# Prologue of a differential-attention layer: modulation rows in two PSUM banks and partly on VectorE, the first weight group among x's tiles

## The reference, cut to what matters

```python
c_act = jax.nn.silu(c)
mod = c_act @ ada_w[0] + ada_b[0]                 # (1, 2048) @ (2048, 6144)
shift, scale, gate = jnp.split(mod, 3, axis=-1)
h = rms_norm(x, norm_pre[0]) * (1.0 + scale[:, None, :]) + shift[:, None, :]
y = diff_attention(h, diff_w_in, diff_w_out, ...)  # h @ diff_w_in first: (1024, 2048) @ (2048, 8192)
x = x + gate[:, None, :] * rms_norm(y, norm_post[0])
```

## Time and profile before

| what | value |
| --- | --- |
| median of 3 runs | 1999.75 us (1997.54 to 2002.05) |
| the profiled execution, own time | 2001.04 us |
| its span, first to last instruction | 1999.1 us |
| TensorE busy (PE) | 1943.5 us, 97% of the span |
| VectorE, ScalarE, GpSimd busy | 1282.0, 786.5 and 567.5 us |
| mean granted TensorE clock | 0.993 of full speed |

### The profile page before, as it was taken

The page is one execution under the profiler, slowest core; times in us unless marked ns, Lnnn a source line. Parts: engine busy times, 40 slices in busy tenths (PEclk is TensorE's granted clock), DMA queues, the critical chain, the costliest instruction groups (busy, mean ns, idle before and its releaser), DMA issues.

```text
span 1999.1 us, 26598 instructions
## 1 busy us (share of the span) xinstructions
PE 1943.5 (97%) x9252; PEld 1586.5 (79%) x9252; DVE 1282.0 (64%) x2096; ACT 786.5 (39%) x1567; POOL 567.5 (28%) x624
## 2 busy tenths in 40 slices
PE   5989999999999999999999999999999989999998
PEld 1368888888888877888888888888888878888886
DVE  1566676666566445778888887888878755534352
ACT  4433333333445332444444444444444434322240
POOL 1123333342456332333242423243332310000000
PEclk9999999999999999999999999999999999999999
DMA  9667666664365777776867777786868675476543
GB/s 327 199 221 242 211 203 204 207 191 142 138 216 200 247 284 242 226 238 200 255 207 238 231 223 229 217 249 207 249 196 256 221 266 167 129 253 201 162 153 85
DMA packets 391489, 426.52 MB, mean 213 GB/s; under 512 B 21078, under 2 KB 287420, under 8 KB 388796
## 3 DMA queue, kind: packets, MB, share of 16 engines
q1 hardware_dynamic: 391072, 424.76, 66.9%
q10 hardware_dynamic: 284, 0.05, 0.0%
HBM read 294.70 MB, written 130.03 MB: 212 GB/s over the span
## 4 chain that ended last, share of the span: by engine, by line
PE 90%; DVE 3%; issue 2%; SPq 2%; DMA 2%; POOL 1%; ACT 1%; DVEq 0%; POOLq 0%; ACTq 0%
PE ps L1545 28%; PE ps L1547 28%; PE ps L1546 28%; PE ps L1533 2%; PE ps L1663 2%; PE ps L1637 1%; POOL sums L724 1%; POOL stg L737 1%; PE ps L1521 1%; SPq L475 1%; PE ps L1682 1%; SPq L364 1%; DMA h_dr<-stg 1%; DVE ring L1110 0%; DMA x2s<-in_x_dram 0%
## 5 line engine op out<-in xcount | busy, mean ns | idle before, releaser
L1545 PE MATMUL ps<-blk,ring 128*128 128x512 f32 x1536 | 609.0, 396 | 11.8 <-ACT cc L889 5.1
L1547 PE MATMUL ps<-blk,ring 128*128 128x512 f32 x1536 | 600.4, 391 | 0.0
L1546 PE MATMUL ps<-blk,ring 128*128 128x512 f32 x1536 | 600.4, 391 | 0.0
L1545 PEld LDWEIGHTS ps<-blk,ring 128*128 128x128 f32 x1536 | 289.6, 189 | 71.9 <-issue 13.6
L1547 PEld LDWEIGHTS ps<-blk,ring 128*128 128x128 f32 x1536 | 289.6, 189 | 61.8
L1546 PEld LDWEIGHTS ps<-blk,ring 128*128 128x128 f32 x1536 | 290.0, 189 | 56.9
L1110 DVE TENSOR_TENSOR ring<-sums,ring 128x512 fp32r<-128x512 f32 x256 | 226.8, 886 | 127.6 <-ACT ring L820 125.4
L724 POOL TENSOR_TENSOR sums<-raw 128x512 f32<-128x512 f32 x128 | 193.1, 1509 | 365.4 <-DVE ring L1110 300.8
L820 ACT ACTIVATE ring<-sums 128x512 fp32r<-128x512 f32 x256 | 159.9, 626 | 177.8 <-PE ps L1547 177.8
L1110 DVE TENSOR_TENSOR ring<-raw,ring 128x512 fp32r<-128x512 f32 x192 | 161.9, 844 | 82.7 <-ACT ring L820 81.7
L724 POOL TENSOR_TENSOR sums<-sums,raw 128x512 f32<-128x512 f32 x128 | 190.9, 1492 | 25.4 <-DVE ring L1110 18.3
(11 more groups left out here) (152 smaller groups left out, 3020.6 us busy)
## 6 DMA issues: line engine op xcount, KB each, us to landing
raw<-in_diff_w_in_dram SPq DMA_DIRECT2D x64, 1024.0 KB, 7.2
d_dr<-cc SPq DMA_DIRECT2D x128, 256.0 KB, 2.8
cc<-d_dr SPq DMA_DIRECT2D x128, 256.0 KB, 4.1
w_raw<-in_diff_w_out_dram SPq DMA_DIRECT2D x128, 256.0 KB, 3.6
ada<-in_ada_w_dram SPq DMA_DIRECT2D x108, 256.0 KB, 4.9
ada<-in_ada_w_dram SPq DMA_DIRECT2D x32, 512.0 KB
q_sb<-q_dr SPq DMA_DIRECT2D x64, 256.0 KB, 3.2
k_sb<-k_dr SPq DMA_DIRECT2D x64, 256.0 KB, 4.3
```

Of the source, the lines that this page charges most:

```text
L1545: MM(dst, a_hi, b_hi, start=start, stop=False, skip_group_check=True)
L1546: MM(dst, a_hi, b_lo, start=False, stop=False, skip_group_check=True)
L1547: return MM(dst, a_lo, b_hi, start=False, stop=stop, skip_group_check=True)
```

## The change

The modulation rows of even chunks go to PSUM bank 4 and those of odd chunks to bank 3 (`ROW_BANK`), so that a chunk's rows wait for `mod_ok` of the chunk before the last one. The transposes of x rotate over banks 5, 6, 7 (`X_BANK`): three of a chunk's four come behind the chunk's last stripe, the fourth behind the second stripe of the next chunk. In chunks 1 to 3 the stripes 1, 3 and 5 of the eight (six of the sixteen 128-row slices) are not multiplied by TensorE: VectorE multiplies and adds them into `acc0` (`rows0`), two instructions a stripe, one stripe behind low 3, one behind low 2 and one behind sum 3 of the chunk before. TensorE adds `acc0` into the row with one matmul with ones (`ada_sum`), ahead of the last stripe. `begin(j)` now comes once in each of chunks 1, 2 and 3, ahead of stripe 6. The load of the first weight group stands ahead of x's tile 4, its four sums on GpSimd behind tiles 4 to 7, and its first four high and low parts behind tiles 5 and 6. ScalarE copies P1 out between high parts 4 and 5 of chunk 3, the products of group 0 wait step by step, and the sums of group 1 wait until low 4 of chunk 3 is done. Stripe s waits for stripe s - 6 through `taken`, which names the engine that used it.

```diff
-    X_BANK = (3, 5, 6, 7)
+    X_BANK = (5, 6, 7)
+    ROW_BANK = (4, 3)
...
+    ON_DVE = (1, 3, 5)
...
+        def on_dve(s):
+            return s >= 8 and s % 8 in ON_DVE
+
+        def taken(s):
+
+            n = sum(not on_dve(r) for r in range(s + 1))
+            return (row_ok, 2 * (s + 1 - n)) if on_dve(s) else (ada_used, n)
...
-                    sp.wait_ge(ada_used, s - ADA_RING + 1)
+                    sp.wait_ge(*taken(s - ADA_RING))
...
             for t in range(TT):
+                if t == HT:
+                    load_raw(0)
                 sp.dma_start(x1[:, :, t, :], x_v[:, t, 0:KP]).then_inc(x_in[t], 16)
                 sp.dma_start(x2s[:, t], x[0, t * P:(t + 1) * P, D // 2:D]).then_inc(x_in[t], 16)
                 load_ada_start(t)
             for s in range(8, 4 * 8):
                 load_ada_start(s)
-                if s == 11:
-                    load_raw(0)
-            sp.wait_ge(ada_used, 30)
+            sp.wait_ge(*taken(28))
+            sp.wait_ge(*taken(29))
             load_raw(1)
...
+                if i == 1 and which == 0:
+                    pool.wait_ge(h_lo_d, 3 * NP + 5)
...
+                if t >= HT:
+                    add_w(0, t - HT)
...
+                if t in (5, 6):
+                    for m in (2 * t - 10, 2 * t - 9):
+                        high_w(m)
...
-                A(h32[:, q // 2, half * HALF:(half + 1) * HALF], ps[:, X_BANK[q] if js < 4 else VX], ACT.Identity,
+                A(h32[:, q // 2, half * HALF:(half + 1) * HALF], ps[:, X_BANK[y % 3] if js < 4 else VX], ACT.Identity,
...
-                if j in (1, 2):
-                    for m in (2 * j - 2, 2 * j - 1):
-                        high_w(m)
-                act.wait_ge(ada_used, 8 * (j + 1))
-                A(mod_row[0:1, :], ps[0:1, SC], ACT.Copy).then_inc(mod_row_ok, 1)
+                act.wait_ge(*taken(8 * j + 7))
+                A(mod_row[0:1, :], ps[0:1, ROW_BANK[j % 2]], ACT.Copy).then_inc(mod_row_ok, 1)
...
+                    if j == 3 and y == 4:
+                        first_out(0)
...
+                if t in (5, 6):
+                    for m in (2 * t - 10, 2 * t - 9):
+                        low_w(m)
+
+            def rows0(s):
+
+                dve.wait_ge(ada0_in[s % ADA_RING], 32 * (s // ADA_RING + 1))
+                for m in range(2):
+                    g, src = 2 * (s % 8) + m, ada_start(s)[:, m]
+                    if g == 2 * ON_DVE[0]:
+                        i = V.tensor_scalar(acc0[:, :], src, cact[:, g:g + 1], None, ALU.mult)
+                    else:
+                        dve.wait_ge(row_ok, taken(s)[1] - 2 + m)
+                        i = STT(acc0[:, :], src, cact[:, g:g + 1], acc0[:, :], ALU.mult, ALU.add)
+                    i.then_inc(row_ok, 1)
+
+            dve.wait_ge(x_sq, 2 * TT)
...
-                if ch in (1, 2):
-                    for m in (2 * ch - 2, 2 * ch - 1):
-                        low_w(m)
...
                 low_h(3)
+                if ch < 3:
+                    rows0(8 * ch + 8 + ON_DVE[0])
                 block_sums(ch, tA, 2)
                 low_h(2)
+                if ch < 3:
+                    rows0(8 * ch + 8 + ON_DVE[1])
                 low_h(4)
                 block_sums(ch, tA, 3)
+                if ch < 3:
+                    rows0(8 * ch + 8 + ON_DVE[2])
                 low_h(5)
                 low_h(6)
...
-                    if y == 0:
-                        pe.wait_ge(cols_ok, 1)
-                        pe.wait_ge(lam_e, 1)
-                    if js:
-                        pe.wait_ge(h_ev, y - 3)
+                    if y >= 3:
+                        pe.wait_ge(h_ev, y - 2)
...
-                if r == 0 and ch:
-                    pe.wait_ge(mod_ok, ch)
+                if s == 8:
+                    pe.wait_ge(cols_ok, 1)
+                    pe.wait_ge(lam_e, 1)
+                if r == 0 and ch >= 2:
+                    pe.wait_ge(mod_ok, ch - 1)
...
-                    i = MM(ps[0:1, SC], cact[:, g:g + 1], ada_start(s)[:, g % 2], start=g == 0, stop=g == TG - 1)
+                    i = MM(ps[0:1, ROW_BANK[ch % 2]], cact[:, g:g + 1], ada_start(s)[:, g % 2], start=g == 0, stop=g == TG - 1)
                 i.then_inc(ada_used, 1)
+
+            def ada_sum(ch):
+
+                pe.wait_ge(row_ok, 2 * len(ON_DVE) * ch)
+                MM(ps[0:1, ROW_BANK[ch % 2]], ones[:, 0:1], acc0[:, :], start=False, stop=False)
...
                 for r in range(8):
-                    ada_rows(8 * ch + r)
-                    if r == (4 if ch else 7):
-                        for q in range(4):
-                            x_turn(4 * ch + q)
+                    if r == 6 and ch:
+                        begin(ch - 1)
+                    if r == 7 and ch:
+                        ada_sum(ch)
+                    if not on_dve(8 * ch + r):
+                        ada_rows(8 * ch + r)
+                    if r == 1 and ch:
+                        x_turn(4 * ch - 1)
+                for q in range(3):
+                    x_turn(4 * ch + q)
                 mod_turn(ch)
-                if ch == 2:
-                    begin(0)
-                    begin(1)
-            begin(2)
+            x_turn(15)
...
-                if i == 0:
-                    pe.wait_ge(h_lo_d, 3 * NP + start_low(pi))
...
                 for j in range(KB - 1 if n in EARLY_PRODUCTS else 0, KB):
+                    if i == 0:
+                        pe.wait_ge(h_lo_d, NP * j + start_low(pi))
                     last = three(ps[:, bank_of(i, pi)], ring[:, n % RING, 0, j], ring[:, n % RING, 1, j],
```

More of the change, by code:

```diff
@@ L156, in build @@
         assert z5_at[0] == base[0]
+        acc0 = at("acc0", [P, AC], F32, [z5_at[0] - (KB * HALF * 4) // KB])
         slotA = blk
@@ L370, in load_ada @@
                 if s == 32:
-                    sp.wait_ge(ada_used, 32)
+                    sp.wait_ge(*taken(29))
+                    sp.wait_ge(*taken(31))
                 if s >= 36:
@@ L703, in _, with add_w @@
             pool.wait_ge(consts, 6)
+            def add_w(i, which):
+                if which == 0:
+                    pool.wait_ge(raw_in[i % 2], 16 * (i // 2 + 1))
+                a11, a12 = raw[:, i % 2, 0::2, 0:P], raw[:, i % 2, 1::2, 0:P]
+                a21, a22 = raw[:, i % 2, 0::2, P:2 * P], raw[:, i % 2, 1::2, P:2 * P]
+                if i:
+                    pool.wait_ge(w_ok, NP * (i - 1) + (P5, P6, P7, P3)[which] + 1)
+                if i == 1 and which == 0:
+                    pool.wait_ge(h_lo_d, 3 * NP + 5)
+                if which in (1, 3):
+                    pool.wait_ge(s_ok, 4 * i + (which + 1) // 2)
+                one, two = ((a21, a22), (sums[:, 0], a11), (a11, a21), (sums[:, 1], a12))[which]
+                TTP(sums[:, which], one, two, ALU.add).then_inc(s_ok, 1)
             for t in range(TT):
@@ L851, in modulate, with first_out @@
                 act.wait_ge(xT_mm, y + 1)
-                A(h32[:, q // 2, half * HALF:(half + 1) * HALF], ps[:, X_BANK[q] if js < 4 else VX], ACT.Identity,
+                A(h32[:, q // 2, half * HALF:(half + 1) * HALF], ps[:, X_BANK[y % 3] if js < 4 else VX], ACT.Identity,
                   scale=mod[:, KT + k:KT + k + 1], bias=mod[:, k:k + 1]).then_inc(h_ev, 1)
-            for j in range(4):
-                if j in (1, 2):
-                    for m in (2 * j - 2, 2 * j - 1):
-                        high_w(m)
-                act.wait_ge(ada_used, 8 * (j + 1))
-                A(mod_row[0:1, :], ps[0:1, SC], ACT.Copy).then_inc(mod_row_ok, 1)
+            def first_out(n):
+                i, pi = divmod(n, NP)
+                b = {P1: C11, P6: C12, P5: C22, P4: C21}[pi]
+                buf = buffer_of(i, b)
+                act.wait_ge(prod, n + 1)
+                if uses[i, b] > 1:
+                    act.wait_ge(d_st[buf], 16 * (uses[i, b] - 1))
+                A(cc[:, buf], ps[:, bank_of(i, pi)], ACT.Copy, scale=-1.0 if pi == P4 else 1.0).then_inc(ev_a, 1)
+            for j in range(4):
+                act.wait_ge(*taken(8 * j + 7))
+                A(mod_row[0:1, :], ps[0:1, ROW_BANK[j % 2]], ACT.Copy).then_inc(mod_row_ok, 1)
                 def high_h(y):
@@ L904, in _ @@
             for n in range(NA):
-                if n and (n - 1) % NP in (P1, P6, P5, P4):
+                if n > 1 and (n - 1) % NP in (P1, P6, P5, P4):
                     first_out(n - 1)
@@ L1520, in x_turn @@
                 for t in range(HT):
-                    i = TR(ps[:, X_BANK[q] if js < 4 else VX, t * P:(t + 1) * P], src[:, k, half * HT + t], ident[:, :])
+                    i = TR(ps[:, X_BANK[y % 3] if js < 4 else VX, t * P:(t + 1) * P], src[:, k, half * HT + t], ident[:, :])
                 i.then_inc(xT_mm, 1)
@@ L1539, in mod_turn @@
                 for b in range(4):
-                    i = MM(ps[:, SC, b:b + 1], mod_row[0:1, b * P:(b + 1) * P], ones[0:1, 0:1], start=True, stop=True)
```

(1 more changed line is left out.)

14 lines of the change are left out of this document (3 added, 11 removed).

## The result

The changed kernel takes 2006.19 us (median of 7 runs, 2004.67 to 2007.86) against 1999.75: a ratio of 1.0026, interval 1.0017 to 1.0036, so 5.2 us slower by the ratio; the two medians lie 6.4 us apart. Its profiled execution took 2004.99 us, with a span of 2003.2. The forecast was no change, 1999.8, with a range from 1994.0 to 2003.5; the measured median lies above it.

What follows compares the result with a forecast made beforehand. TensorE, busy 1943.5 of 1999.1 us, bounds the kernel, so only its prologue waits can be won. Start +3.6, chunks -4.2, clock +3.2 and end -2.6 sum to 0.0: 1999.8 us, range 1994.0 to 2003.5.

Steps and rivals of the forecast that it cites:

- Start: Prologue up to M0: load +3.0, fewer transposes -0.5, tile 7's scaling beside GpSimd's sum +1.1; +3.6 us in all.
- M0: Start of chunk 0's first modulate, ending its rows, turn and bias; forecast to move from 46.58 to 50.2.
- Chunks: Three periods between chunks' first modulates: 54.0 instead of 58.25 us, -4.2; two clock falls of 1.6 add +3.2.
- VectorE's chain of 12.45: In each period VectorE's row operations end 12.45 us after the chunk's first modulate; TensorE idles 3.6 us for them.
- End: From M3 to P7's start: 12.4 us instead of 14.97, -2.6, with P7 waiting for its low weights.
- M3: Start of chunk 3's first modulate, at 104.83 before the change; the end stretch is counted from it.
- S: Marker for the prologue's end, chosen after measuring: ScalarE's copy of P4 of group 0, 128.27 before; not in the prediction.
- The clock as a rival: TensorE's clock falls in all three periods and the end stretch: 1.6 + 1.6 on top, 2003.0 us; chance 0.04.
- lower bound of 10.45: End stretch: earliest P7 start, M3 + 10.45, without GpSimd's sums delaying VectorE's last low parts.
- The ring: Chunks: forecast has stripes 15, 23, 31 landing in time; rival has them late, +7.8 in all, 2007.6 us, chance 0.08.
- GpSimd's lock: GpSimd's sums block VectorE on a shared port: +1.07 at tile 7's scaling, 1.07 per sum at the last low parts.
- two outer cases: Clock holds and GpSimd stays clear: 1993.6, chance 0.30 with neighbours; clock low in all periods and end: 2003.0, chance 0.04.

Runs made afterwards that it cites:

- fill: Changed kernel with four more matmuls, results unused, between stripe 6 and the sum in each of chunks 1 to 3; ratio 1.0009 to the kernel before.
- pool_late: Changed kernel, but GpSimd's sums of weight group 1 wait for the low part of P7's weights; ratio 1.0011 to the kernel before.
- copy_early: Changed kernel, but VectorE copies P2 out behind sum 3 of chunk 3, ahead of low part 5; ratio 1.0014 to the kernel before.
- two_stripes: Changed kernel with two stripes of eight (1 and 3) on VectorE instead of three; ratio 0.9982 to the kernel before.
- changed_again: The changed kernel timed and profiled once more, with no edit; ratio 1.0027 to the kernel before (12 runs).
- tuned_warm_end: Changed kernel with two_stripes, pool_late, copy_early, no sum behind tile 7, and 19 unread matmuls in end-stretch gaps; ratio 0.9959 to the kernel before.

## Why the prediction was wrong

- **Start, forecast +3.6, measured +4.5.** The load's 3.0, the scaling's +1.0 and the shorter transposes are right. The rest is when x lands in an execution: with the early load ScalarE starts on tile 7 at 41.60 to 43.73, against 41.84 from the sum (38.79 before, plus 3.05). And there is one thing the sum had no term for: in four executions (fill, pool_late, copy_early, two_stripes) the clock fell during the last stripe of chunk 0, the transposes took 1.3 us longer and the turn 0.8, and M0 was at 52.1 to 53.2. In changed_again M0 is at 52.16 for another reason, tiles that landed 1.9 us later than the sum has them.
- **Chunks, forecast 54.0 and 3.2 for the clock, measured 58.0.** A period without a fall is 18.2 instead of 18.0, a fall costs 1.65 instead of 1.6, and there are two. VectorE's chain of 12.45 was 12.5. TensorE reached the sum later than forecast and idled for 3.1 us instead of 3.6. Right, 0.8 us too low in sum; that the profiled execution had just two falls was luck, since changed_again had three and pool_late one.
- **End, forecast -2.6, measured +0.4.** This is the step that failed: "P7's low weights at 12.4, and P7 starts at M3 + 12.4". Its first half was right (M3 + 12.4), its second wasn't (M3 + 14.4). I let P7 wait only for its weights and passed over P5's last step between them, which waits for P2's copy by VectorE, one place behind those weights. That wait put P5's step at M3 + 13.1. S - M3 is 22.25 with it, and 21.0 without it in pool_late and copy_early, where the forecast amounts to 12.4 + 128.27 - 119.80 = 20.9: 1.3 us for the wait. It also made an idle time of 1.98, behind which the clock fell in the profiled execution: 23.86 instead of 22.25, 1.6 more. The two are the 3.0.
- **The clock as a rival** was weighed for the three periods and "the end stretch", with 0.04. It was no rare case: TensorE has short idle times in the whole changed prologue, and falls were seen in the last stripe of chunk 0, in two thirds of the periods, from P2's last step (or before it) into P6 in every profile of a changed kernel but tuned_warm_end's, and behind P6 in four of eight. The prediction took P6 to run at 2.4 GHz; in pool_late, without GpSimd's sums, P6 at 1.2 GHz is what holds P7 to M3 + 12.1, so its lower bound of 10.45 was out of reach.
- **The ring** was no matter, as forecast. **GpSimd's lock** was as forecast in both places. The Trainium skill (SBUF — State Buffer, "SBUF: two separate sides") has a block for the length of the other's instruction; the trace agrees, to 0.2 us, for a scaling of one input: 1.75 us beside a sum of 1.26 against 0.75 alone, where a block to the sum's end would give 1.94.
- **The range** ran from 1994.0 to 2003.5, while its two outer cases had been worked out as 1993.6 and 2003.0; the half microsecond at either end has no working.

Sum by S: 0.0 forecast, +4.7 measured, of it 0.9 start, 0.8 chunks, 3.0 end. The timed runs have +5.2 by the ratio (0.26% of 2000) and +6.4 by the medians. The split rests on one profiled execution of each kernel, and where the remaining 0.5 to 1.7 us come from is open.

## What to carry to other kernels

When a wait is shortened, list every wait of the next instruction in the queue, also of the small ones between two big steps: the one that was long met before the change may be the last after it. Work shifted from the bounding engine should stop where the two chains meet (two stripes here, not three), because an idle time on TensorE can be paid twice, once as the wait and, in 12 of 16 cases here, once more in the clock. And a transfer or a sum moved out of one stretch has to be priced where it lands.

## What was not expected of the hardware

- An idle time of 3.1 us on TensorE between dense work was followed by 1.2 GHz in 12 of 16 cases and by 2.4 GHz in the others, with the same instructions before it (in two more periods it was only 1.75, and no fall followed); idle times of 2.7 us between x's stripes were followed by 1.2 GHz within the next stripe in 19 of 24 cases over all profiles, and those of 1.8 to 2.0 us ahead of P5's last step by a fall in four of eight. Which, changes from one execution to the next.
- Matmuls with one output row, whose results are dropped, held the clock at 2.4 GHz ahead of the sum in all three periods of fill; the two periods that began at 2.4 GHz took 18.4 us against 19.9 with a fall.
- The prologue's gain or loss isn't carried one to one into the time: the changed kernel's S is 4.7 later and its span 4.1 longer, fill's S 5.6 later and its span only 1.4 longer (2000.5 against 1999.1). From S to the end it is 1870.2 to 1873.8 us in thirteen of the fourteen profiled executions, and 1866.7 in fill's, so one profile's S tells a difference in the time only to a few us. The difference arises behind the prologue, and its cause was not tried.
